# Attention by groups of heads that share a PSUM bank, and a latent attention whose first projection and modulation are moved

## The reference

```python
# hybrid: 8 heads of 64, 256 keys, ALiBi slopes; beside it a gated delta rule in chunks
logits = logits - slopes[None, :, None, None] * dist[:, None]
p = jax.nn.softmax(jnp.where(valid[:, None], logits, NEG_INF), axis=-1)
# latent attention: 16 heads of 96 (64 + 32 rotated), values of 64, 256 keys
c_q, c_kv, k_rope = jnp.split(u @ w_in, [384, 640], axis=-1)
q = (rms_norm(c_q, q_norm_g) @ w_q_up).reshape(bsz, seq, 16, 96)
kv = (rms_norm(c_kv, kv_norm_g) @ w_kv_up).reshape(bsz, seq, 16, 128)
# mixer: 4 causal heads (moba); 4 heads over compressed (15 keys), selected and window keys; GLA
p = masked_softmax(jnp.concatenate([s_sel, s_own], axis=-1), mask).astype(v.dtype)
return gates[..., 0:1] * o_cmp + gates[..., 1:2] * o_slc + gates[..., 2:3] * o_win
o_gla = gla_attention(heads(gq, 4), heads(gk, 4), heads(gv, 4), heads(log_a, 4))
z = g_a * (o_moba @ w_branch_moba) + g_b * (o_nsa @ w_branch_nsa) + g_c * (o_gla @ w_branch_gla)
```

## Time and profile before

| what | value |
|---|---|
| median of 3 runs | 2470.86 us (2465.46 to 2471.58) |
| profiled execution, its own time | 2470.93 us |
| its span, first to last instruction | 2469.1 us |
| PE busy | 2240.8 us (91%) |
| DVE / ACT / POOL busy | 1388.5 / 1035.0 / 287.3 us (56 / 42 / 12%) |
| mean granted clock of PE | 0.925 |

### The profile page before, as it was taken

The page is one execution under the profiler, slowest core; times in us unless marked ns, Lnnn a source line. Parts: engine busy times, 40 slices in busy tenths (PEclk is TensorE's granted clock), DMA queues, the critical chain, the costliest instruction groups (busy, mean ns, idle before and its releaser), DMA issues.

```text
span 2469.1 us, 31110 instructions
## 1 busy us (share of the span) xinstructions
PE 2240.8 (91%) x12416; PEld 1827.9 (74%) x12416; DVE 1388.5 (56%) x2086; ACT 1035.0 (42%) x1741; POOL 287.3 (12%) x396
## 2 busy tenths in 40 slices
PE   4999889989999999699999789897999889897999
PEld 2777788667777777577778677665998777666997
DVE  2654767656457556456555473447565484445663
ACT  2344453335444443365443343343554343343552
POOL 0000200112002000222100131130000131130000
PEclk8999989999999999899999898858999898868999
DMA  9677633458757864465565443204565544213664
GB/s 296 202 250 236 167 103 88 160 170 265 252 201 248 263 230 151 142 199 191 197 197 196 122 144 101 94 14 137 167 185 183 143 138 124 63 37 117 180 185 139
DMA packets 374497, 412.17 MB, mean 167 GB/s; under 512 B 27511, under 2 KB 319563, under 8 KB 374352
## 3 DMA queue, kind: packets, MB, share of 16 engines
q1 hardware_dynamic: 367216, 388.37, 50.8%
q0 software_dynamic: 7136, 21.81, 2.7%
HBM read 407.49 MB, written 2.62 MB: 166 GB/s over the span
## 4 chain that ended last, share of the span: by engine, by line
PE 76%; DVE 10%; ACT 4%; POOL 3%; DMA 2%; issue 2%; SPq 2%; DVEq 0%; POOLq 0%; ACTq 0%
PE ps L169 73%; PE ps L172 3%; DVE wlo L178 2%; SPq L220 2%; DVE arena L178 2%; DVE arena L190 1%; ACT whi L175 1%; ACT arena L175 1%; DMA raw<-in_ffn_w_up 1%; POOL tmp L178 1%; DVE tmp L178 1%; POOL arena L220 1%; POOL small L178 1%; DVE tmp L190 1%; ACT uh L175 0%
## 5 line engine op out<-in xcount | busy, mean ns | idle before, releaser
L178 DVE TENSOR_TENSOR wlo<-raw,whi 128x1024 fp32r<-128x1024 f32 x592 | 720.7, 1235 | 458.5 <-ACT whi L175 456.6
L175 ACT ACTIVATE whi<-raw 128x1024 fp32r<-128x1024 f32 x592 | 606.8, 1049 | 341.0 <-DMA raw<-in_w_up 87.2
L169 PE MATMUL ps<-whi,uh 128*128 128x512 f32 (+2 forms) x1298 | 539.9, 416 | 55.9 <-DVE wlo L178 15.1
L169 PE MATMUL ps<-wlo,uh 128*128 128x512 f32 (+2 forms) x1298 | 518.6, 400 | 0.0
L169 PE MATMUL ps<-whi,ul 128*128 128x512 f32 (+2 forms) x1298 | 413.6, 394 | 0.0
L169 PE MATMUL ps<-whi,arena_r 128*128 128x512 f32 x1184 | 372.6, 393 | 0.0
L169 PEld LDWEIGHTS ps<-whi,uh 128*128 128x128 f32 x1298 | 254.7, 196 | 139.1 <-issue 38.4
L175 ACT ACTIVATE arena<-ps 128x256 f32<-128x256 f32 (+8 forms) x297 | 121.5, 414 | 445.8 <-PE ps L169 381.6
L169 PE MATMUL ps<-arena 128*128 128x128 f32 (+7 forms) x1360 | 269.0, 346 | 36.0 <-DVE arena L190 8.7
L169 PE MATMUL ps<-uh,whi 128*128 128x256 f32 x984 | 286.1, 291 | 12.9 <-DVE arena L190 6.6
L169 PEld LDWEIGHTS ps<-whi,ul 128*128 128x128 f32 x1298 | 252.1, 194 | 53.0
(11 more groups left out here) (190 smaller groups left out, 1859.0 us busy)
## 6 DMA issues: line engine op xcount, KB each, us to landing
arena<-in_mod_w SPq DMA_DIRECT2D x60, 1024.0 KB, 5.8
raw<-in_w_in SPq DMA_DIRECT2D x90, 512.0 KB, 3.6
raw<-in_ffn_w_gate SPq DMA_DIRECT2D x176, 256.0 KB, 4.0
raw<-in_ffn_w_up SPq DMA_DIRECT2D x176, 256.0 KB, 4.7
raw<-in_ffn_w_down SPq DMA_DIRECT2D x88, 512.0 KB, 3.4
raw<-in_w_up SPq DMA_DIRECT2D x88, 512.0 KB, 3.9
raw<-in_w_down SPq DMA_DIRECT2D x44, 512.0 KB, 4.4
raw<-in_hyb_w_in SPq DMA_DIRECT2D x32, 512.0 KB, 3.9
```

What stands on the lines that cost most here:

```text
L169: return Nothing() if self.raw is None else self.raw.matmul(out, l, r, start=start, stop=stop)
L175: return Nothing() if self.raw is None else self.raw.activation(out, src, func, **kw)
L178: return Nothing() if self.raw is None else self.raw.tensor_tensor(out, a, b, op)
```

## The change

1. **Groups.** `units` become `groups`. The logits of two heads with 256 keys, or of four heads with 128 or 15 keys, fill one bank of 512 columns; one add, one maximum (a column for each head), one PT copy, one power on POOL and one output for the group. The exponentials with their sums stay one for each head, but for the compressed keys (one subtraction, one exponential, one sum on DVE). All outputs are DVE's. Hybrid 16 units -> 8 groups, latent attention 32 -> 16, each mixer 32 -> 11. `L` buffers: 3, 3 (was 4), 3 (was 4), now 512 columns wide; `PT` two in all three (was 3). So lag 2 and lag2 3 everywhere: 20 -> 11, 37 -> 19, 37 -> 14 steps. Where two neighbours in a group sit on different row halves of the array, PE waits for its own earlier matmul (`at_row`).
2. **Latent attention.** `c1` goes with `c0` by token halves. Six of the 12 modulation groups leave the attention: four stand in front of `ct`, one behind it, one in `mlaq`; SP opens them earlier. The first bias part of that stage is loaded before the attention.

```diff
-def attend_steps(n, room):
+def attend_steps(room):
     lag = len(room["L"]) - 1
     return lag, lag + len(room["PT"]) - 1
...
@@ pe_attend
-            pe.matmul(bank[:, 0:u["k"].shape[1]], u["q"], u["k"], True, True).then_inc(*pe.ev("at_s", tag, i))
+            for m, (q, k, _) in enumerate(g["items"]):
+                if m and q.base_partition() != g["items"][m - 1][0].base_partition():
+                    last.then_inc(*pe.ev("at_row", tag, i))
+                    pe.wait_ge(*pe.on("at_row", tag, i))
+                last = pe.matmul(bank[:, m * g["w"]:(m + 1) * g["w"]], q, k, True, True)
+            last.then_inc(*pe.ev("at_s", tag, i))
@@ act_attend
-            act.activation(lb, lb, ACT.Exp, bias=sc[:, 0:1], accum_out=sc[:, 1:2]).then_inc(*act.ev("at_e", tag, i))
+                for m, place in enumerate(places(g)):
+                    x = lb[:, m * g["w"]:(m + 1) * g["w"]]
+                    last = act.activation(x, x, ACT.Exp, bias=att_cols(M, i, g, "max")[:, m:m + 1],
+                                          accum_out=att_cols(M, i, g, "sum")[:, place:place + 1])
@@ dve_attend
+            if "after" in g:
+                dve.wait_ge(*dve.on("at_out", tag, g["after"]))
+                for m in range(n):
+                    last = dve.stt(g["dst"][:, m, :], o[:, m, :], inv[:, m:m + 1], g["dst"][:, m, :], ALU.mult, ALU.add)
+            else:
+                last = dve.tt(g["dst"], o, inv.unsqueeze(2).broadcast_to([P, n, 64]), ALU.mult)
...
@@ class Hybrid
-        self.units = []
-        for h in range(8):
+        self.groups = []
+        for h0 in (0, 1, 4, 5):
             for t in range(T):
...
-MLA_MODS = tuple(range(1, 37, 3))
+MLA_MODS = tuple(range(1, 19, 3))
...
@@ pe_mla
-    pe_tok_halves(pe, M, [("c0", L.w, 0, 512, (4, 5), lambda t: [("pj_act", "c0", t)])], 3, second_half)
-    pe_tok(pe, M, "c1", L.w, 512, 672, M.uT, KD, ready, lambda t: ("pj_act", "c1", t))
+    pe_tok_halves(pe, M, [("c0", L.w, 0, 512, (4, 5), lambda t: [("pj_act", "c0", t)]),
+                          ("c1", L.w, 512, 672, (6, 7), lambda t: [("pj_act", "c1", t)])], 3, second_half)
+    mark(pe, M, 4, "up")
+    pe_mod(pe, M, 3)
+    pe_mod(pe, M, 2)
+    pe_mod_sum(pe, M, 1)
+    pe_mod_sum(pe, M, 0)
+    pe_mod(pe, M, 3)
+    pe_mod(pe, M, 2)
     pe_flip(pe, M, "ct", L.cb, 5, (0, 1, 2), [pe.on("mla_v", "norm", 1)], lambda j: [("flip_dve", "ct", j)])
+    pe_mod(pe, M, 3)
     ct = [pe.on("flip_dve", "ct", 2)]
     for c in range(3):
+        if c:
+            pe_mod_sum(pe, M, 1)
+            pe_mod_sum(pe, M, 0)
+        if c == 1:
+            pe_mod(pe, M, 3)
...
@@ act_mla
-    act_unit(act, M, 4)
-    act_tok(act, M, "c1", KD, 160, keep(("c1",), lambda t: L.cb[:, t, 512:672]))
+        act.wait_ge(*tok_made(act, M, "c1", t))
+        act.activation(L.cb[:, t, 512:672], M.bank(6 + t)[:, 0:160], ACT.Copy).then_inc(*act.ev("pj_act", "c1", t))
+    for b in (3, 2, 3, 2):
+        act_mod(act, M, b)
+    act_unit(act, M, 6)
...
@@ class Mixer
-        self.room = dict(L=[M.lngb[:, 0, i * S:i * S + S] for i in range(4)], PT=[area(T, P) for _ in range(3)], banks=((6, 7), (2,), (3,)))
-        self.units = []
+        self.room = dict(L=[M.lngb[:, 0, 0:512], M.lngb[:, 0, 512:1024], area(512)], PT=[M.vis.rearrange("p t s -> p (t s)"), M.dist.rearrange("p t s -> p (t s)")],
+                         banks=((6, 7), (2,), (3,)))
+        self.groups = []
...
@@ sp_program, the branch of the latent attention
+            sp_mods_open(sp, M, n, sp.on("used", M.uid[("s", 3), "y"]))
+            sp_upto(sp, M, n, "up")
+            for _ in range(MLA_FRONT - 2):
+                sp_mods_next(sp, M)
             sp_upto(sp, M, n, "out")
-            sp_mods_open(sp, M, n, sp.on("flip", "mkT", 7))
+            sp.wait_ge(*sp.on("flip", "mkT", 7))
```

More of the change, by code:

```diff
@@ L750 @@
 N_MOD = 72
+MLA_FRONT = 6
 def stage_groups(n):
@@ L1235, in pe_attend, with places, att_cols @@
+def places(g):
+    return (0, 2, 1, 3) if len(g["items"]) == 4 else range(len(g["items"]))
+def att_cols(M, i, g, what):
+    at = ("max", "sum", "inv").index(what) * 4
+    return M.att[i % 6][:, at:at + len(g["items"])]
+def pe_attend(pe, M, tag, groups, room, need):
+    lag, lag2 = attend_steps(room)
     sb, tb, vb = room["banks"]
-    for i in range(len(units) + lag2):
+    for i in range(len(groups) + lag2):
         if i >= lag2:
             j = i - lag2
-            u = units[j]
-            bank = fill(pe, M, vb[j % len(vb)], (u["out"], tag, j))
+            g = groups[j]
+            tiles, rows = key_tiles(g)
+            bank = fill(pe, M, vb[j % len(vb)], ("at_out", tag, j))
@@ L1279, in act_attend @@
             j = i - lag
-            w = units[j]["k"].shape[1]
-            js, b = -(-w // P), min(P, w)
+            g = groups[j]
+            tiles, rows = key_tiles(g)
+            n = len(g["items"]) * tiles * P
             act.wait_ge(*act.on("at_t", tag, j))
@@ L1326, in dve_attend, with pool_attend @@
         yield
-def pool_attend(pool, M, tag, units, room):
-    lag, lag2 = attend_steps(len(units), room)
-    for i in range(len(units) + lag2):
-        if lag <= i < len(units) + lag:
+def pool_attend(pool, M, tag, groups, room):
+    lag, lag2 = attend_steps(room)
+    for i in range(len(groups) + lag2):
+        if lag <= i < len(groups) + lag:
             j = i - lag
-            u, sc = units[j], M.att[j % 6]
-            pool.wait_ge(*pool.on("at_e", tag, j))
-            over = pool.tt(sc[:, 2:3], sc[:, 1:2], M.minus, ALU.pow)
-            if "gate" in u:
+            g = groups[j]
+            n, inv = len(g["items"]), att_cols(M, j, g, "inv")
+            pool.wait_ge(*(pool.on("at_n", tag, j) if "keep" in g else pool.on("at_e", tag, j)))
+            over = pool.tt(inv, att_cols(M, j, g, "sum"), M.minus.broadcast_to([P, n]), ALU.pow)
+            if "gate" in g:
@@ L2122, in pe_chosen @@
     need = [pe.on("pj_dve", "k", 2), pe.on("pj_act", "v", 1)]
-    yield from pe_attend(pe, M, "hyb", H.units, H.room, need)
+    yield from pe_attend(pe, M, "hyb", H.groups, H.room, need)
 def act_chosen(act, M, H):
@@ L2128, in act_chosen @@
         yield
-    yield from act_attend(act, M, "hyb", H.units, H.room)
+    yield from act_attend(act, M, "hyb", H.groups, H.room)
 def dve_chosen(dve, M, H):
@@ L2135, in dve_chosen @@
     dve.wait_ge(*dve.on("ix_ma", 1))
-    yield from dve_attend(dve, M, "hyb", H.units, H.room)
+    yield from dve_attend(dve, M, "hyb", H.groups, H.room)
 def pool_chosen(pool, M, H):
@@ L2141, in pool_chosen @@
         yield
-    yield from pool_attend(pool, M, "hyb", H.units, H.room)
-MLA_MODS = tuple(range(1, 37, 3))
+    yield from pool_attend(pool, M, "hyb", H.groups, H.room)
+MLA_MODS = tuple(range(1, 19, 3))
 class Mla:
@@ L2261, in act_mla @@
             act_flip(act, M, tag, j, 16, dst, (4, 5, 6, 7), width=96)
-    for i, _ in enumerate(act_attend(act, M, "mla", L.units, L.room)):
+    for i, _ in enumerate(act_attend(act, M, "mla", L.groups, L.room)):
         if i in MLA_MODS:
@@ L2327, in dve_mla @@
             dve_flip(dve, M, tag, j, 16, dst, (4, 5, 6, 7), width=96)
-    for i, _ in enumerate(dve_attend(dve, M, "mla", L.units, L.room)):
+    for i, _ in enumerate(dve_attend(dve, M, "mla", L.groups, L.room)):
         if i in MLA_MODS:
@@ L2902, in act_softmaxes @@
     yield from blank(3)
-    yield from act_attend(act, M, ("mix", n), X.units, X.room)
+    yield from act_attend(act, M, ("mix", n), X.groups, X.room)
 def dve_softmaxes(dve, M, X):
@@ L2961, in dve_softmaxes @@
     dve.copy(X.kcT, M.bank(3)[:, 0:N]).then_inc(*dve.ev(q, "kcT", n))
-    yield from dve_attend(dve, M, ("mix", n), X.units, X.room)
+    yield from dve_attend(dve, M, ("mix", n), X.groups, X.room)
 def pool_softmaxes(pool, M, X):
@@ L2980, in pool_softmaxes @@
     yield
-    yield from pool_attend(pool, M, ("mix", n), X.units, X.room)
+    yield from pool_attend(pool, M, ("mix", n), X.groups, X.room)
 def pe_pairs(pe, M, X, lv, q, k, *ready):
```

243 lines of the change are left out of this document (139 added, 104 removed).

## The result

The changed kernel takes **2452.53 us** (median of 4 runs, 2449.06 to 2454.93) against 2470.99 us before (median of 4, 2465.46 to 2471.58): a ratio of 0.9929, with an interval of 0.991 to 0.9948. It is faster by 18 us (0.7%, clear of the noise but small), where 44 were forecast, and lies above the range of 2400 to 2448.

What follows compares the result with a forecast made beforehand. PE was taken as the bound, mostly with untouched projections, the gain lying in two half-clock mixer drains. From 2470.93 us: mixers -50, hybrid +9, latent attention -3, giving 2426.9 us; range 2400 to 2448.

Steps and rivals of the forecast that it cites:

- Mixers, the cover: Mixer attention between projection pieces: 3866 more columns done before the last projection, costing 6.3 us per mixer.
- the price of 1.64 ns: PE's cost per streamed column at full clock, taken from unit starts 1.05 us apart in the latent attention; 3.28 at half.
- Mixers, the drain: Last projection to the 16 transposes: near 37 us in place of 68.7, at granted clock 0.50.
- in lag 2: Mixer drains: a group's 2.6 us add, maximum and exponentials hide behind PE steps of 3.4 to 4.9 us.
- Hybrid: Hybrid's end: late bias load behind POOL's head norm, then queued sums and fixes, start `O` transposes 9 us later.
- Latent attention: Six fewer modulation groups inside, -9.8 us; stalls and longer end, +3.3; front, +3.5; sum 3 us less.
- Full clock in the drains: Rival: the mixer drains return to full clock, saving 33 us each, total 2411 us; chance 0.20.
- Rule and rows: Mixer drains: skill's rule says busy PE regains full clock; the trace showed 0.50 while 91% busy, and the forecast followed it.
- The hybrid without loss: Rival: the hybrid loses nothing, as head norm starts earlier or the queue is short; 2415 us; chance 0.12.
- Overhead by instructions: Rival: mixer overhead goes with instructions and changes of kind, not steps; 7.5 us more per mixer, 2442 us; chance 0.15.
- The chain as bound: Rival: DVE, ACT and POOL work bounds the mixer drains, 2.8 us more a step; 2477 us or more; chance 0.03.

Runs made afterwards that it cites:

- e4_single: The changed kernel with experiment 1's flag fix, each mixer head a group of its own except for compressed keys; 2466.33 us.
- e6_norm: Experiment 3's kernel, with DVE doing the head norm's squares and sums of both token halves in one step; 2433.97 us.
- e9_delay: Also experiment 9: e6_norm with both mixers' attention begun one background step later, moving one four-head group from cover to drain; 2426.53 us.
- experiments 1 and 2: 1: changed kernel, background-tick flag set to the same value at each mixer's start, 2441.78 us; 2: kernel before, flag turned at first mixer's start, 2477.72 us.
- Experiment 3: Experiment 1's kernel, with the hybrid's yields for modulation at every second tick in place of every third; 2433.32 us.
- experiment 6: Experiment 3's kernel, with two of three ticks given to GLA where two backgrounds run, so GLA is done before the last projection; 2445.99 us.
- experiment 5: The run e4_single: experiment 1's kernel with mixer heads one to a group, except for compressed keys; 2466.33 us.
- experiment 8: e6_norm with a third PT buffer in the mixers, one step more; 2438.03 us.

## Why the prediction was wrong

To see what a stretch is made of, cut PE's time into slices of half a us. In each, the profile gives PE's busy time and the granted clock. Idle time is what is not busy; "clock" is the busy time times one less the granted clock, which is what full clock would have saved; the rest is PE's own work at full clock. These are estimates, summed from windows of the traces:

| us | cover | idle | clock | work | drain | idle | clock | work |
|---|---|---|---|---|---|---|---|---|
| before, mixer 1 | 38.4 | 3.8 | 5.1 | 29.4 | 68.7 | 9.4 | 28.2 | 31.1 |
| before, mixer 2 | 38.4 | 3.8 | 5.1 | 29.4 | 67.8 | 10.2 | 26.2 | 31.4 |
| after, mixer 1 | 52.0 | 6.2 | 7.8 | 38.0 | 36.2 | 10.2 | 7.6 | 18.4 |
| after, mixer 2 | 55.2 | 6.2 | 11.3 | 37.7 | 36.2 | 10.2 | 7.6 | 18.4 |
| `e4_single`, mixer 1 | 39.3 | 4.0 | 3.4 | 31.9 | 62.0 | 11.2 | 23.3 | 27.5 |
| `e6_norm`, mixer 1 | 51.5 | 6.2 | 7.4 | 37.9 | 33.2 | 7.2 | 7.6 | 18.4 |
| `e9_delay`, mixer 1 | 41.2 | 3.1 | 1.7 | 36.5 | 41.5 | 5.8 | 15.2 | 20.5 |

The work column hardly differs between executions of one order of work; the clock column does. The change took 4.1 and 4.8 us of work out of the two mixers, and added 3.2 and 2.3 us of idle time. The rest of its gain there is clock, 18.0 and 12.4 us, as work went from a drain at half clock to a cover mostly at full clock.

**Mixers, the cover: the step that failed.** "The 3866 more cost 6.3 us there, at the full-clock price, since that part ran at 0.86." They cost 13.6 and 16.8 us, from three terms. The work is 8.6 and 8.2 us (2.1 to 2.2 ns a column), not 6.3: the price of 1.64 ns came from another attention. PE's idle time grew by 2.4 us, most of it the wait at GLA's first chunk. And 2.6 and 6.2 us went to half clock, where the prediction assumed that the cover's clock stays. I had priced PE's own work under cover, and had looked at DVE's and ACT's queues at GLA's last chunk only, not at its first, where the first step with four heads stands between a weight split and the chunk. Experiment 9 moves that one group: the idle time goes, and the cover's half clock with it, though not for good (the drain then loses as much). That the group's place causes both is shown; that the longer wait is what lowers the clock is not. The kernel before fell to half clock behind a wait of 2.1 us and stayed there for 10 us; `e9_delay` did so for 3 us behind one of 2.3.

**Mixers, the drain.** Forecast 37.3 us, found 36.2 in both. That it came out right is luck: two parts of the sum were off and met in the middle. The clock was 0.68, not 0.5, worth about 11 us: PE ran at full clock behind the last projection, fell to half in the wait for GLA's last chunk, came back to full as that chunk ended, and fell again at the wait of 1.49 us. Against it, 3.5 us were lost to the head norm and 3.1 to ACT's PT copies, which were not in the sum, and the work was more. The chain of a group does not hide "in lag 2": with two PT buffers it shows between transposes and values.

**The parity.** Nothing in the prediction had it. The sum said that the 146 us ahead of the first mixer's attention do not change, since no line of them does. It cost 6.7 us (experiments 1 and 2), 15% of the forecast gain.

**Hybrid.** Right, by its steps: head norm to 526.8 (forecast 527), fix at 531.0 (533), `O` at 539.9 (540). The last two groups took 3.7 us each, dearer than the 2.2 that I took: the clock was 0.50 there, from inside the wait of 10.88 us on. The fix came 2 us earlier. Experiment 3 shows the cause.

**Latent attention.** Forecast -3, found near 0 (0.1 with two FFNs, whose own variation is as large). The attention gained 3.4 us, not 6.5: PE's work fell by 7.7 us, not 9.8, idle time rose by 3.4 and half clock cost 0.9 more. PE's stalls were up to 0.97 us each at ACT's PT copy, where I had 0.4 at the logits' chain. In front, PE waits 6.97 and 4.21 us for loads; counted from the end of the layer norm ahead, `ct` is 1.7 us later.

**Rivals.** Full clock in the drains: half true, 0.68, and worth what the waits then cost. Rule and rows: experiment 6 has PE busy for 36.88 of 37.0 us at 0.50, so the rule of the Trainium skill, TensorE: Matmul & The Clock Gate, "Part 1", that a busy engine gets its full clock back, does not describe this fp32 attention. What it is in this work that keeps the clock down is open; the latent attention, with 96 rows in place of 64, runs at 0.94 to 1.00. The hybrid without loss: false. Overhead by instructions: false for PE's instructions (experiment 5), not told apart for changes of kind. The chain as bound: it shows in the waits for ACT listed above, but at 0.8 to 1.5 us, not 2.8 us a step. What `at_row` costs, and the latent attention's `c1` by token halves, no run tests alone.

## What to carry to other kernels

A step of background work costs what PE streams for it, what its longest queue delays, and what the clock then loses: before making steps larger, look at what stands behind them on ACT and DVE at each place where PE waits, and move a step if two waits meet. When steps get fewer and larger, count everything that goes by their number: yields that carry other work, flags that alternate, and what they reorder in sub-layers that the edit does not touch. Read every stretch of the profile after, also those that the diff leaves alone. And don't read a price per column from two stretches at different clocks: split them into idle time, clock and work first.

## What the runs showed of the hardware

PE at half clock with no gap: 36.88 us busy of 37.0 at a granted clock of 0.50, in 64-row logits, transposes and 64-column values in fp32 (experiment 6). The same kind of groups ran at full clock in other places. Windows of the changed kernel's second mixer, columns as in the earlier trace rows: groups behind the last projection; GLA's last chunk, behind a wait of 3.67 us; the groups behind that chunk; what follows the wait of 1.49 us; and, from the cover, a stretch of projection and GLA, ahead of which PE had been busy for 14.89 of 15.0 us.

```profile
2151.40:2156.60 5.20, 5.20 (x33) 3.84 (x31) 1.80 (x3) 2.30 (x7) 0.00 (x0) 1.00 0.30 101
2160.30:2164.00 3.70, 3.70 (x14) 3.34 (x14) 1.57 (x3) 1.09 (x4) 0.81 (x2) 0.50 0.02 4
2164.60:2169.30 4.70, 4.70 (x29) 3.54 (x28) 2.24 (x6) 1.54 (x5) 0.00 (x0) 0.98 0.00 0
2170.80:2187.40 16.60, 11.55 (x48) 9.50 (x49) 5.35 (x13) 3.98 (x11) 9.71 (x11) 0.53 0.00 0
2130.80:2133.80 3.00, 3.00 (x10) 2.44 (x9) 0.91 (x2) 2.03 (x9) 0.30 (x1) 0.50 0.02 5
```

So the clock came back in the drain without a projection, behind GLA's 128-row, 256-column matmuls, and it fell once with PE busy throughout. In `e9_delay` it did not come back behind the same chunk. In the latent attention of the changed kernel it fell behind a wait of 2.2 us and came back after 7 us, among the groups themselves. Removing the wait of 1.49 us did not keep the clock up in experiment 8 (from 2158.8 to 2173.1 us `e6_norm`, which has that wait, ran at 0.50). These traces show when the clock changed and what PE did before; they do not give one rule for it.
